# TensorE's place in a gather pipeline: a mark's own pairs taken at once at chosen marks, one more pair right behind new rows, and the first norm's rows behind the output projection

## The chip, the core and the metric

The kernel runs on one NeuronCore of a Trainium2 chip. The metric is the device time of one launch in microseconds (us), the median of several executions. The engines are called PE (TensorE), DVE (VectorE), ACT (ScalarE), POOL (GpSimd, which here does nothing but issue gathers) and SP (SyncE, which issues the weight loads).

## What is computed

One decoder layer over 1024 tokens of width 1024, all in float32: a combined input projection, sliding-window attention and a gated DeltaNet side by side, an output projection, a LayerNorm, then PEER (a product-key lookup of single-neuron experts), and a second LayerNorm.

```python
def reference(x, positions, w_in, ..., peer_w_query, peer_sub_keys, peer_u, peer_v, ln2_g, ln2_b):
    mix = hybrid_mixer(h, positions, w_in, attn_sinks, conv_w, a_log, dt_bias, dn_norm_g, w_out)
    h = layer_norm(DEEPNORM_ALPHA * h + mix, ln1_g, ln1_b)
    ffn = peer_ffn(h, peer_w_query, peer_sub_keys, peer_u, peer_v)
    h = layer_norm(DEEPNORM_ALPHA * h + ffn, ln2_g, ln2_b)

def one_block(xb):                       # 128 tokens
    q = (xb @ w_query).reshape(L, PEER_HEADS, 2, PEER_QUERY_DIM // 2)
    s = jnp.einsum('lhpd,hpkd->lhpk', q, sub_keys)
    vals, idx = lax.top_k(s, K)          # 16 of 128, for 8 heads x 2 halves
    ...
    best, pos = lax.top_k(cand, K)       # 16 of the 256 sums
    expert = jnp.take_along_axis(cidx, pos, axis=-1)
    gate = jax.nn.softmax(best, axis=-1)
    u = expert_u[expert]                 # 128 tokens x 128 experts x 1024
    v = expert_v[expert]
    h = jax.nn.gelu(jnp.einsum('ld,lhkd->lhk', xb, u), approximate=False)
    return jnp.einsum('lhk,lhkd->ld', (h * gate).astype(xb.dtype), v)
```

Every token has 128 experts of its own, and each brings a row of `u` and a row of `v`, 8 KB together. For all tokens that is 1.07 GB, which has to be gathered from memory.

## The kernel before

**Blocks.** The 1024 tokens are 8 blocks (`NB`) of 128. For each block all engines walk through the same function `mix(n, ...)`, each with its own part: rotary positions, attention, DeltaNet, output projection, first norm, queries, key scores and the choice of experts ("routing", on DVE, in four rounds `i` = 0 to 3). Weights come in 23 chunks of 1 MB, four of which stay in SBUF (`KEPT`); the other 19 are loaded anew for each block through two buffers (`chunk`), each load issued when PE has used the chunk two before it (`chunk_used`).

**Gathers.** A block has 128 gathers (`SLOTS`), one per choice of expert, each of 128 rows of 8 KB: 1 MB. POOL issues them in order into a ring of 8 places (`RING`), which is four pairs. Gather `j` may go out when PE has added gather `j - 8` (`added`), and the first of each 32 when DVE has written the expert numbers (`staged`, written in `expert_used`). 

**Pairs.** Two gathers are one pair (64 per block, `PAIRS`). For a pair DVE makes two dot products of the `u` rows with the tokens (L1421, the `CUSTOM_DVE` rows, `ring<-ring,x_pair`), ACT turns them by gelu and gate into a diagonal matrix (L994, L997, L1001, `diag`), and PE multiplies this with the `v` rows and sums in PSUM (L757, `expert_sum<-ring,diag`, eight instructions in the profile for a pair). Only then are two places of the ring free.

**Marks.** How pairs are woven into the mixer is a table. Each engine calls `mark(name)` at the same named steps, and there it does the pairs that the table gives to this name. `EARLIER` names the steps of block n at which pairs of block n-1 are done (49 pairs), `OWN` the later ones, from `top1` on, at which the block's own first 15 pairs are done, while routing goes on and PE already does the input projection of block n+1 (`in_chunk(n + 1, c)`). DVE and ACT do a mark's own pairs. PE stays one pair behind: its function is called with `b - 1`.

```python
def __call__(self, name):
    pairs, count = (self.own, OWN[name]) if name in OWN else (self.earlier, EARLIER[name])
    if pairs:
        pairs(self.done, self.done + count)
    self.done += count
```

**The turn from one block's pairs to the next's.** At `pick0` the first 32 expert numbers of the new block are there, and POOL may issue. PE does the last pair of the old block (`turn_over`), the four rows of the second norm's gain and shift (L514, `ln_row`, broadcast over the partitions by a matmul), and goes on. DVE waits for PE's last sum, reads the sums out of PSUM (`read_sums`, L1439), copies the gates into pair order (`by_pair`, L1401) and the new tokens' rows into `x_pair` (`stage_rows`, L1410). Pairs of the new block need `x_pair`.

**First norm.** Its gain and shift are spread by PE in the same way (`ln_row(LN1_G, ...)`, `ln_row(LN1_B, ...)`, L514), between the last DeltaNet step (mark `kv1`) and mark `dn`. Then PE waits for DVE's `dn_out`, transposes (L504), and does four output chunks (L485) with a mark behind each, `out0` to `out3`. DVE adds the residual, takes the statistics, asks ACT for the root, scales (needs the gain rows) and shifts (needs the shift rows).

## Time and profile before

| | us |
|---|---|
| median of 3 runs | 3309.68 |
| lowest, highest | 3298.28, 3327.20 |
| profiled execution, its own time | 3315.64 |
| profiled execution, span from first to last instruction | 3313.6 |

The page of the profile gives busy time by engine (PE 2454.9, DVE 2231.1, ACT 1142.5, POOL 1180.1 us) and says that 1254 MB were moved in 174885 packets, 379 GB/s over the span. Its DMA line shows the share of time in which the 16 DMA engines were busy, and its GB/s line what they moved. The two must be read together with a stretch in which the DMA engines never pause: there the same engines move 420 GB/s.

### The profile page before, as it was taken

What the parts mean: (1) busy time and instruction counts of PE and PEld (TensorE: products, weight loads), DVE (VectorE), ACT (ScalarE), POOL (GpSimd) and SP (SyncE); (2) the same over time, 40 slices, a digit from 0 to 9 for tenths busy, and PEclk for the clock granted to TensorE, in tenths of its full rate; (3) what the DMA queues carried; (4) which work ended last, traced back from release to release, by engine and by line L of the source; (5) the groups of instructions that cost most, each with busy time, mean ns of one, the idle gap of its engine ahead of it and who ended that gap; (6) DMA issues with size and microseconds to landing.
All of it is one profiled execution on the core that took longest, in us unless ns stands there. A gap on an engine that the chain in (4) does not pass through costs nothing.

```text
span 3313.6 us, 37482 instructions
## 1 busy us (share of the span) xinstructions
PE 2454.9 (74%) x11840; PEld 1381.2 (42%) x11840; DVE 2231.1 (67%) x5593; ACT 1142.5 (34%) x3499; POOL 1180.1 (36%) x1028
## 2 busy tenths in 40 slices
PE   7776778867888577876788677886788866775554
PEld 6663335533455233542346333552345523341111
DVE  3267765886558765687657876588656876569444
ACT  3213532235332443326232353233533253322222
POOL 0022443234432353224432344323453244323443
PEclk8788888988899898998989888997899879887777
DMA  8049999999999999999999999999999999989997
GB/s 327 7 198 405 393 419 399 378 389 411 408 385 412 379 408 405 382 406 382 420 395 378 400 391 407 400 392 389 411 407 397 402 390 417 389 356 351 419 420 316
DMA packets 174885, 1254.22 MB, mean 379 GB/s; under 512 B 20184, under 2 KB 20312, under 8 KB 23520
## 3 DMA queue, kind: packets, MB, share of 16 engines
q0 software_dynamic: 147456, 1073.81, 79.8%
q1 hardware_dynamic: 25056, 172.66, 12.6%
q10 hardware_dynamic: 2176, 5.36, 0.4%
q8 instruction: 95, 1.56, 0.2%
q14 instruction: 102, 0.84, 0.1%
HBM read 1247.56 MB, written 4.19 MB: 378 GB/s over the span
## 4 chain that ended last, share of the span: by engine, by line
DMA 33%; PE 33%; DVE 17%; ACT 9%; issue 5%; POOL 2%; ACTq 0%; DVEq 0%; POOLq 0%; SPq 0%
DMA ring<-in_uv,expert_used 21%; PE expert_sum L757 13%; DMA chunk<-in_weights 12%; PE bank L493 8%; DVE ring L1421 8%; PE bank L485 6%; ACT diag L1001 2%; POOL ring L445 2%; PE bank L499 1%; PE bank L586 1%; ACT L994 1%; ACT arena L861 1%; PE bank L504 1%; ACT h_raw L994 1%; DVE conv L1168 1%
## 5 line engine op out<-in xcount | busy, mean ns | idle before, releaser
L445 POOL DMA_INDIRECT ring<-in_uv,expert_used x1024 | 1179.9, 1152 | 2102.8 <-PE expert_sum L757 1600.8
L757 PE MATMUL expert_sum<-ring,diag 128*64 128x512 f32 x4096 | 1212.5, 721 | 646.0 <-ACT diag L1001 645.6
L1421 DVE CUSTOM_DVE_ANT_0 ring<-ring,x_pair 128x1024 f32<-128x1024 f32 x1024 | 1231.7, 1223 | 586.3 <-DMA ring<-in_uv,expert_used 581.3
L757 PEld LDWEIGHTS expert_sum<-ring,diag 128*64 128x64 f32 x4096 | 314.7, 156 | 1290.4 <-issue 1275.7
L994 ACT ACTIVATE h_raw<-h_raw 128x2 f32<-128x2 f32 x512 | 104.3, 204 | 1531.9 <-DVE h_raw L1421 1531.1
L1001 ACT ACTIVATE diag<-const,h_raw 128x64 f32<-128x64 f32 x1024 | 292.7, 332 | 0.0
L997 ACT ACTIVATE h_raw<-h_raw,gate_used 128x1 f32<-128x1 f32 x1024 | 245.6, 286 | 16.8
L493 PE MATMUL bank<-oT,chunk 128*128 128x128 f32 x1824 | 224.0, 282 | 33.0 <-DMA chunk<-in_weights 32.1
L493 PEld LDWEIGHTS bank<-oT,chunk 128*128 128x128 f32 x1824 | 213.3, 196 | 66.5 <-DMA chunk<-in_weights 39.6
L493 PE MATMUL bank<-o_cat,chunk 128*128 128x128 f32 x1376 | 172.4, 286 | 40.8 <-DMA chunk<-in_weights 40.6
L493 PEld LDWEIGHTS bank<-o_cat,chunk 128*128 128x128 f32 x1376 | 164.7, 200 | 76.6 <-DMA chunk<-in_weights 48.1
L1144 DVE MAX8 arena<-arena 128x8 f32<-128x128 f32 (+1 forms) x384 | 103.7, 325 | 46.5 <-ACT arena L953 41.3
L499 PEld LDWEIGHTS bank<-arena 128*128 128x128 f32 x768 | 97.7, 204 | 57.9 <-issue 50.8
L499 PE MATMUL bank<-arena 128*128 128x128 f32 x768 | 109.3, 295 | 5.5 <-DVE arena L1286 1.6
L949 ACT COPY arena<-bank 128x512 f32<-128x512 f32 x32 | 18.8, 586 | 265.2 <-PE bank L493 265.2
L485 PE MATMUL bank<-chunk,o_cat 128*128 128x256 f32 x352 | 86.4, 401 | 15.4 <-DMA chunk<-in_weights 15.4
L994 ACT ACT_TABLE_LOAD x72 | 92.4, 1283 | 3.8 <-DVE h_raw L1421 2.5
L485 PEld LDWEIGHTS bank<-chunk,o_cat 128*128 128x128 f32 x352 | 68.7, 200 | 36.7 <-issue 27.2
L1421 DVE DVE_READ_ACCUMULATOR2_ANT h_raw<- 128x1 f32 x1024 | 83.8, 82 | 0.0
L485 PE MATMUL bank<-kept,o_cat 128*128 128x256 f32 x256 | 74.3, 454 | 7.9 <-DMA kept<-in_weights 7.9
L1168 DVE SCALAR_TENSOR_TENSOR conv<-conv_in,conv_w,conv 128x128 f32<-128x128 f32 x288 | 77.7, 343 | 0.0
L485 PEld LDWEIGHTS bank<-kept,o_cat 128*128 128x128 f32 x256 | 58.0, 233 | 34.1 <-issue 22.9
(237 smaller groups left out, 2482.8 us busy)
## 6 DMA issues: line engine op xcount, KB each, us to landing
chunk<-in_weights SPq DMA_DIRECT2D x137, 1024.0 KB, 9.8
ring<-in_uv,expert_used POOLq DMA_INDIRECT x1024, 11.8
ring<-in_weights SPq DMA_DIRECT2D x15, 1024.0 KB, 20.3
o_cat<-in_xT SPq DMA_DIRECT2D x8, 512.0 KB, 11.7
kept<-in_weights SPq DMA_DIRECT2D x4, 1024.0 KB, 19.1
x<-in_x SPq DMA_DIRECT2D x8, 512.0 KB, 12.9
out<-oT ACTq DMA_DIRECT2D x8, 512.0 KB
sub_keys<-in_sub_keys ACTq DMA_DIRECT2D x1, 1024.0 KB
```

Source lines behind the costliest of these rows:

```text
L445: pool.indirect_dma_start(out=ring[:, (j % RING) * 2 * D:(j % RING + 1) * 2 * D], out_offset=None, in_=io["uv"], in_offset=bass.IndirectOf ...
L485: mm = pe.matmul(out, act[:, k, :], w[:, k, :], start=(k == 0), stop=(k == KT - 1))
L493: mm = pe.matmul(out, w[:, k, i * P:(i + 1) * P], act[:, k, :], start=(k == 0), stop=(k == KT - 1))
L499: mm = pe.matmul(out[:, hs], lhsT[:, hs], rhs[:, hs], start=True, stop=True)
L504: mm = pe.transpose(out[:, h * P:(h + 1) * P], in_[:, h * P:(h + 1) * P], ident)
L757: mm = pe.matmul(expert_sum[i][c * SPAN:(c + 1) * SPAN, :], diag[:, (j % DIAGS) * SPAN:(j % DIAGS + 1) * SPAN], ring3[:, j % RING, D + i * ...
L994: act.activation(h_raw[:, pair[0]:pair[1] + 1], h_raw[:, pair[0]:pair[1] + 1], ACT.Gelu).then_inc(gelued.sem, 1)
L997: act.activation(h_raw[:, j:j + 1], h_raw[:, j:j + 1], ACT.Copy, scale=gate_used[:, j:j + 1]).then_inc(weighted.sem, 1)
L1001: act.activation(diag[:, (j % DIAGS) * SPAN:(j % DIAGS + 1) * SPAN], C["halves"], ACT.Copy, scale=h_raw[:, j:j + 1]).then_inc(diag_ready.s ...
L1144: ins = dve.max(values[:, one[part]], one[2])
L1168: stt(out=convo[:, t, :], in0=conv3[:, t, k:k + P], scalar=conv_w[:, t * TAPS + k:t * TAPS + k + 1], in1=convo[:, t, :], op0=ALU.mult, op1 ...
L1421: dve.tensor_tensor_reduce(u, u, x_pair[:, (j % 2) * D:(j % 2 + 1) * D], 1.0, 0.0, ALU.mult, ALU.add, h_raw[:, j:j + 1]).then_inc(dotted.s ...
```

## The change

- `Marks` gets a list `prompt`. At a mark in this list PE does all pairs up to and with the mark's own; at any other mark it does all pairs before the mark's own and none of them. The list `PROMPT` has `gates, scores, taps2, norms, kv1, out0` to `out3, scale1, half_q, qu0` and all marks of `OWN`. DVE and ACT do what the table says, as before.
- The table: `dn` has one pair instead of two, and `OWN` has a new first mark `turned` with one pair, directly behind `turn_over` on DVE. PE does `in_chunk(n + 1, 0)` ahead of it.
- PE's turn: the last old pair comes ahead of the fourth key scores, not behind.
- DVE's turn: `by_pair` and half of the copies into `x_pair` (the half that `read_sums` doesn't read) are done before the wait for PE's last sum.
- The first norm's rows are made behind the fourth output chunk, ahead of mark `out3`.
- `diag` gets eight places instead of four; a constant, `same64`, is dropped for it, and one small matmul becomes two.

```diff
-DIAGS = 4
+DIAGS = 8
...
-    merge64=1, solve=2, ws0=1, kv0=2, ws1=1, kv1=1, dn=2, o_T=1, out0=1, out1=1, out2=1, out3=1,
+    merge64=1, solve=2, ws0=1, kv0=2, ws1=1, kv1=1, dn=1, o_T=1, out0=1, out1=1, out2=1, out3=1,
...
-OWN = {name: 1 for name in ("top1",) + NEXT_IN + AFTER_IN}
+OWN = {name: 1 for name in ("turned", "top1") + NEXT_IN + AFTER_IN}
+PROMPT = ("gates", "scores", "taps2", "norms", "kv1", "out0", "out1", "out2", "out3", "scale1", "half_q", "qu0") + tuple(OWN)
...
         if pairs:
-            pairs(self.done, self.done + count)
+            pairs(self.done, self.done + (count if name in self.prompt else 0))
...
-                pe.wait_ge(late_in, late)
                 pe.wait_ge(*o_copied.at(n, 2))
-                ln_row(LN1_G, 0, ln1_rows)
-                ln_row(LN1_B, 1, ln1_rows)
...
                     tokens_out(n, IN_CHUNKS + c, bank[3 + c // 2][:, (c % 2) * W:(c % 2 + 1) * W], oTv, early)
+                    if c == OUT_CHUNKS - 1:
+                        pe.wait_ge(late_in, late)
+                        ln_row(LN1_G, 0, ln1_rows)
+                        ln_row(LN1_B, 1, ln1_rows)
                     mark(f"out{c}")
...
                 mark("pick0")
+                turn_over(n)
                 score_keys(3)
-                turn_over(n)
+                second_norm_rows(n)
+                if onward:
+                    in_chunk(n + 1, 0)
+                mark("turned")
                 mark("top1")
-                for c, name in enumerate(NEXT_IN):
-                    if onward:
+                for c, name in enumerate(NEXT_IN, 1):
+                    if onward and c < IN_CHUNKS:
                         in_chunk(n + 1, c)
                     mark(name)
...
-            mix(0, Marks(own=lambda a, b: experts(0, b - 1)), lambda n: None, early=True)
+            mix(0, Marks(own=lambda a, b: experts(0, b), prompt=PROMPT), lambda n: None, early=True)
...
             def turn_over(n):
 
-                dve.wait_ge(*chunk_used.at(n, CHUNKS))
-                read_sums(n - 1)
-                stage_rows(n)
+                if n > 0:
+                    dve.wait_ge(*added.at(n - 1, 2 * PART))
+                by_pair(gate_used, gate, 0, PART)
+                stage_rows(n, False)
+                if n > 0:
+                    dve.wait_ge(*chunk_used.at(n, CHUNKS))
+                    read_sums(n - 1)
+                stage_rows(n, True).then_inc(rows_staged.sem, 1)
```

**Where instructions stand.** First PE, from the last DeltaNet matmul of a block to the first query chunk. L673/L674 are the DeltaNet output, L757 (after: L763) pairs, L514 the norm's rows, L504 transposes, L485 output chunks, L493 a query chunk; a pair is x4 here. Before:

```order
L674 MATMUL bank<-conv,arena 128x128
L757 MATMUL expert_sum<-ring,diag 64x512 x4
L514 MATMUL bank<-k_keys,const 128x512 x4
L757 MATMUL expert_sum<-ring,diag 64x512 x8
L504 MATMUL bank<-const,o_cat 128x128 x8
L757 MATMUL expert_sum<-ring,diag 64x512 x4
L485 MATMUL bank<-kept,oT 128x256 x8
L757 MATMUL expert_sum<-ring,diag 64x512 x4
L485 MATMUL bank<-kept,oT 128x256 x8
```

After:

```order
L675 MATMUL bank<-conv,arena 128x128
L763 MATMUL expert_sum<-ring,diag 64x512 x8
L504 MATMUL bank<-const,o_cat 128x128 x8
L763 MATMUL expert_sum<-ring,diag 64x512 x4
L485 MATMUL bank<-kept,oT 128x256 x8
L763 MATMUL expert_sum<-ring,diag 64x512 x8
L485 MATMUL bank<-kept,oT 128x256 x8
```

Between the DeltaNet and the transposes two pairs stand instead of three, and no rows; behind the first output chunk stand two pairs instead of one.

Second PE, at the turn, from the last query chunks to the second chunk of the next block's input projection (L718, after L720, are key scores; `o_cat` is the next block's input). Before:

```order
L493 MATMUL bank<-oT,chunk 128x128 x32
L757 MATMUL expert_sum<-ring,diag 64x512 x4
L718 MATMUL bank<-sub_keys,arena 128x128 x4
L757 MATMUL expert_sum<-ring,diag 64x512 x4
L514 MATMUL bank<-k_keys,const 128x512 x4
L485 MATMUL bank<-kept,o_cat 128x256 x8
L757 MATMUL expert_sum<-ring,diag 64x512 x4
L485 MATMUL bank<-kept,o_cat 128x256 x8
```

After:

```order
L493 MATMUL bank<-oT,chunk 128x128 x32
L763 MATMUL expert_sum<-ring,diag 64x512 x8
L720 MATMUL bank<-sub_keys,arena 128x128 x4
L514 MATMUL bank<-k_keys,const 128x512 x4
L485 MATMUL bank<-kept,o_cat 128x256 x8
L763 MATMUL expert_sum<-ring,diag 64x512 x8
L485 MATMUL bank<-kept,o_cat 128x256 x8
```

The last old pair moved ahead of the key scores, and two new pairs stand between the first two input chunks instead of one. Later in the same run PE has five pairs in a row, not four, ahead of the transposes of `rope`.

Third DVE at the turn (L1439, after L1447, reads the sums; L1144 to L1153, after L1153 to L1162, are the first half of routing round 1). Before:

```order
L1392 TENSOR_TENSOR gate<-gate,small 128x32
L1439 SCALAR_TENSOR_TENSOR oT<-x_pair,expert_sum 64x512 x4
L1401 COPY gate_used<-gate 64x16 x4
L1410 COPY x_pair<-x 64x1024 x4
L1144 MAX arena<-arena 128x8 x4
L1151 MAX_INDEX arena<-arena 128x8 x4
L1153 MATCH_REPLACE arena<-arena 128x128 x4
L1421 ISA ring,h_raw<-ring,x_pair 128x1024
```

After:

```order
L1402 TENSOR_TENSOR gate<-gate,small 128x32
L1411 COPY gate_used<-gate 64x16 x4
L1418 COPY x_pair<-x 64x1024 x2
L1447 SCALAR_TENSOR_TENSOR oT<-x_pair,expert_sum 64x512 x4
L1418 COPY x_pair<-x 64x1024 x2
L1429 ISA ring,h_raw<-ring,x_pair 128x1024
```

The gate copies and two row copies moved ahead of the sums, and the first new pair ahead of the routing.

## Rows read from the trace of the kernel before

**Rows 1.** The page: busy time by engine
```profile
PE 2454.9 (74%) x11840; PEld 1381.2 (42%) x11840; DVE 2231.1 (67%) x5593; ACT 1142.5 (34%) x3499; POOL 1180.1 (36%) x1028
```

**Rows 2.** Windows over blocks: engines' busy us, PE clock, DMA share, GB/s
```profile
592.83:2946.12 2353.29, 1798.11 (x8882) 1021.37 (x8880) 1662.64 (x4177) 862.43 (x2628) 883.94 (x768) 0.89 0.98 398
206.32:592.83 386.51, 294.35 (x1482) 168.64 (x1480) 268.20 (x677) 138.37 (x428) 144.47 (x128) 0.88 0.98 402
...
2946.12:3075.00 128.88, 72.97 (x224) 22.75 (x224) 108.07 (x328) 32.74 (x111) 46.81 (x44) 0.71 0.89 341
```

**Rows 3.** Windows within one block (gathers of block 3 and the next turn)
```profile
1395.00:1426.00 31.00, 24.81 (x123) 15.89 (x121) 29.58 (x95) 9.84 (x27) 7.95 (x7) 0.93 0.98 379
1426.00:1504.00 78.00, 51.67 (x278) 31.27 (x279) 63.95 (x210) 26.02 (x80) 22.14 (x22) 0.88 1.01 420
1504.00:1515.00 11.00, 11.00 (x44) 5.12 (x43) 10.82 (x30) 4.70 (x18) 4.29 (x5) 0.79 0.56 205
...
1674.00:1700.00 26.00, 26.00 (x108) 15.33 (x105) 10.59 (x19) 6.88 (x27) 11.45 (x10) 0.90 0.98 377
...
1769.90:1792.00 22.10, 19.32 (x80) 12.79 (x80) 12.78 (x42) 3.50 (x8) 8.71 (x8) 0.84 0.94 376
1792.00:1827.00 35.00, 30.42 (x171) 20.36 (x172) 33.50 (x106) 13.12 (x38) 10.82 (x10) 0.90 0.91 349
```

**Rows 4.** Who waited for whom: us in total, times, longest
```profile
POOL ring L445 <- PE expert_sum L757: 1600.8, 442, 15.1
```

**Rows 5.** Timeline of PE behind the own pairs: start, us, idle before
```profile
1502.79 1.89 PE L548 MATMUL bank<-const,arena 128*64 128x128 f32 x8 [7.95 <-DVE arena L1188]
...
1505.04 7.08 PE L757 MATMUL expert_sum<-ring,diag 128*64 128x512 f32 x24
```

**Rows 6.** Timeline of ACT and POOL at the same place
```profile
1498.68 0.57 ACT L1001 ACTIVATE diag<-const,h_raw 128x64 f32<-128x64 f32 x2
...
1509.49 0.94 POOL L445 DMA_INDIRECT ring<-in_uv,expert_used  x1 [10.66 <-PE expert_sum L757]
```

**Rows 7.** Timeline of DVE and PE from DeltaNet's end to the queries
```profile
1661.97 3.70 PE L514 MATMUL bank<-k_keys,const 8*128 8x512 f32 x8
...
1673.29 3.68 PE L757 MATMUL expert_sum<-ring,diag 128*64 128x512 f32 x8 [4.11 <-ACT diag L1001]
...
1680.84 3.72 PE L485 MATMUL bank<-kept,oT 128*128 128x256 f32 x16
...
1690.01 1.94 PE L757 MATMUL expert_sum<-ring,diag 128*64 128x512 f32 x8
...
1734.45 1.94 PE L757 MATMUL expert_sum<-ring,diag 128*64 128x512 f32 x8
...
1668.94 0.69 DVE L1316 TENSOR_TENSOR o_cat<-arena,small 128x512 f32<-128x512 f32 x1
...
1683.03 0.57 ACT L1001 ACTIVATE diag<-const,h_raw 128x64 f32<-128x64 f32 x2
...
1725.03 0.57 ACT L1001 ACTIVATE diag<-const,h_raw 128x64 f32<-128x64 f32 x2
```

**Rows 8.** Timeline of PE and DVE at the turn
```profile
1784.30 5.41 PE L485 MATMUL bank<-kept,o_cat 128*128 128x256 f32 x16
1794.31 3.68 PE L757 MATMUL expert_sum<-ring,diag 128*64 128x512 f32 x8 [4.60 <-ACT diag L1001]
...
1780.90 2.78 DVE L1439 SCALAR_TENSOR_TENSOR oT<-x_pair,expert_sum 64x512 f32<-64x512 f32 x4 [7.88 <-PE expert_sum L757]
...
1784.44 2.79 DVE L1410 COPY x_pair<-x 64x1024 f32<-64x1024 f32 x4
...
1790.50 1.23 DVE L1421 CUSTOM_DVE_ANT_0 ring<-ring,x_pair 128x1024 f32<-128x1024 f32 x1
```

**Rows 9.** Timeline of POOL at the turn
```profile
1769.90 1.17 POOL L445 DMA_INDIRECT ring<-in_uv,expert_used  x1 [15.67 <-DVE expert_used L1401]
...
1798.76 1.07 POOL L445 DMA_INDIRECT ring<-in_uv,expert_used  x1 [15.06 <-PE expert_sum L757]
```

More of the change, by code:

```diff
@@ L762, in experts @@
                                 mm.then_inc(added.sem, 1)
-                taken[0] = last
+                taken[0] = max(taken[0], last)
             def second_norm_rows(n):
-                pe.wait_ge(*key_scores_c.at(n, 4))
+                if n == 0:
+                    return
+                if n < NB:
+                    pe.wait_ge(*key_scores_c.at(n, 4))
                 ln_row(LN2_G, 2, ln2_rows)
@@ L974, in mix @@
                 key_scores_out(3)
+                mark("turned")
                 mark("top1")
-                for c, name in enumerate(NEXT_IN):
+                for c, name in enumerate(NEXT_IN, 1):
                     if onward:
@@ L1383, in mix @@
                         turn_over(n)
+                        mark("turned")
                 weights_out(n, 2, slice(2, PH))
@@ L1402, in by_pair, with stage_rows @@
                 return ins
-            def stage_rows(n):
-                by_pair(gate_used, gate, 0, PART)
-                dve.wait_ge(*sums_read.at(n, 0))
+            def stage_rows(n, own):
                 for s in range(2):
-                    for c in range(2):
-                        ins = dve.tensor_copy(x_pair[s * SPAN:(s + 1) * SPAN, c * D:(c + 1) * D], x1[c * SPAN:(c + 1) * SPAN, :])
-                ins.then_inc(rows_staged.sem, 1)
+                    c = s if own else 1 - s
+                    ins = dve.tensor_copy(x_pair[s * SPAN:(s + 1) * SPAN, c * D:(c + 1) * D], x1[c * SPAN:(c + 1) * SPAN, :])
+                return ins
             def experts(n, first, last):
@@ L1441, in read_sums @@
                 ins.then_inc(sums_read.sem, 1)
+                dve.wait_ge(*sums_read.at(n, 1))
             def second_stats(n):
```

24 lines of the change are left out of this document (11 added, 13 removed).

## The prediction, made before the changed kernel ran

> **What bounds the kernel now.** I read the busy times first: no engine is busy for more than 74% of the span [rows 1], so none is the bound. Then the windows. Where the DMA engines never pause they move 420 GB/s, in the window of 78 us [rows 3]. Over the six blocks from 592.83 to 2946.12 us it is 398 GB/s [rows 2]. So gathers and weights bound the kernel, and what can be won at unchanged traffic is the time in which the DMA engines run dry: 2353.29 x (1 - 398/420) = 123 us, 20.5 per block. In the first block it is 386.51 x (1 - 402/420) = 16.6, and in the first 129 us of the last block's gathers 128.88 x (1 - 341/420) = 24.2 [rows 2].
>
> Next, where in a block they run dry. The same sum for windows of one block [rows 3]: 1395 to 1426, behind the turn, 3.0 us (and 5.9 at the next turn, 1792 to 1827; mean 4.5); 1504 to 1515, between the own pairs and the next block's attention, 5.6; 1674 to 1700, output projection, 2.7; 1769.90 to 1792, the new block's first gathers, 2.3. Together 15.1 of the 20.5. Small dips elsewhere make up the other 5.4, and I count no gain for them.
>
> Then who holds the ring. POOL waited 1600.8 us for PE's sums [rows 4]. Mostly that is harmless, since gathers already out keep the engines busy. It costs when the four pairs' worth of cover (8 MB, 20 us at 420 GB/s) is used up. A pair that PE takes later than ACT has it ready shortens this cover by so much.
>
> **The change, part by part.** I call a stretch's dry time its shortage.
>
> *Own pairs' end (shortage 5.6).* ACT had the last own pair's matrices ready at 1499.25 [rows 6], but PE, one pair behind, takes it only at `rope`. It waits 7.95 us for DVE's rotated rows and reaches the pair at 1505.04 [rows 5]. POOL's next gather goes out at 1509.49, after 10.66 us [rows 6], and just there the rate is 205 GB/s [rows 3]. Now the pair is taken at `pick3`. Even at the slow 3.68 us for a pair after idling [rows 8] its places are free at about 1503, so the gather goes out some 6 us earlier. On top of this the own part has 16 pairs instead of 15, so one more gather pair (5.0 us of traffic at 420 GB/s) is already out. 6 + 5 is more than 5.6; I take 5.0 back, because later gathers follow at DVE's pace.
>
> *The turn (shortage 4.5).* DVE idles 7.88 us for PE's last sum, then reads 2.78, copies gates, copies rows 2.79, does half a routing round, and starts the first new pair at 1790.50 [rows 8]. The gate copies (0.7, the gap between the two rows) and half of the row copies (1.4) go into those 7.88 us, and the routing (3.2, from 1787.3 to 1790.5) comes behind the pair. The first new pair starts at 1780.90 + 2.78 + 1.4 = 1785.1, 5.4 us earlier. PE takes it behind last sum, scores, norm rows and one chunk; it stood waiting 4.60 us for this pair [rows 8], after two chunks of 2.7 each at 5.41 for both. So PE can be there at about 1788.5, when ACT is ready as well. The first freed place goes to POOL about 5 us before 1798.76 [rows 9]. Each later own pair is one mark ahead too, at the price of one pair more (2.4 us) on a DVE that is busy for 33.50 of 35 us there [rows 3]. 5 against a shortage of 4.5: I take 3.5. Moving the last old pair ahead of the key scores gains DVE little, since ACT's matrix for it was the wait. The fourth scores come about 3 us later, and only routing round 3 reads them, far behind.
>
> *First gathers (shortage 2.3).* They wait for DVE's expert numbers, 15.67 us up to 1769.90 [rows 9], and nothing in routing is taken out. But DVE does pairs between its steps and waits for their landing. PE takes the pair ready at 1725.60 only at 1734.45 [rows 7]; with `half_q` prompt it does so behind the first query chunk, some 5 us sooner, and a later gather leaves sooner too. Against it, the second query chunk starts 1.94 us later, and at `qu0` PE may wait some 2 us for ACT. I take 1.0, between nothing and 2.3.
>
> *Output projection (shortage 2.7).* PE does the norm's rows (3.70) and two pairs and waits 4.11 us for the second, so the transposes start at 1673.29 + 3.61 = 1676.9, though DVE's `o_cat` was there at 1669.6 [rows 7]. Now one of these pairs and the rows are gone from there, and `dn` takes nothing of its own: the transposes can start 7 us earlier. Behind the output chunks the lag goes: a pair ready at 1683.60 was taken at 1690.01 [rows 7], 6.4 us late. The rows' 3.70 us now lie behind the fourth chunk, where DVE adds a residual half, takes statistics, does one pair and waits for ACT's root before it wants them; nothing is exposed, and if this cover were gone it would be 3.70. I take 2.0.
>
> *The rest.* Eight places of `diag`: ACT's wait for a free one does not show in the trace, so 0. One more small matmul per block: under 0.3 us, in PE's wait. DVE's added wait for its own sums: 0.1. In the own part itself the list changes nothing but names: the order of in-chunks and pairs is the same, one pair ahead.
>
> *Sum.* 5.0 + 3.5 + 1.0 + 2.0 = 11.5 per block, 69 for six. The first block has no turn from old pairs but the other three: 8. In the last block's beginning no weights flow and the spacing of DVE's marks keeps the rate down; it has the turn and an extra early pair: 6. Together 83 us. From the profiled execution's 3315.64 (span 3313.6 and 2.0 around it) that gives 3233. It lies 6 us over the median of the runs, 3309.68, with which the result is compared: 3309.7 - 83 = **3227**.
>
> **A rule of the skill weighed.** The pages give this traffic another bound: the Trainium skill, "DMA: Bandwidth & Descriptors", section Bandwidth, says that some 358 GB/s per core bind between memory and SBUF. By that the DMA engines would have no dry time and the change would give 0. The trace disagrees, with 420 GB/s over 78 us, so it gets no chance.
>
> **The rivals.**
> 1. *The chain of the engines is next.* Gathers leave earlier, but a stage is then as long as DVE's and PE's work in it. For it: DVE's 33.50 of 35 us behind the turn. Against it: PE's and DVE's waits for rows that stand all over the block. Half of the gain stays: 3309.7 - 42 = 3268.
> 2. *Nearly all shortages go*, since being one pair ahead carries into stretches I counted at nothing: 17 of 20.5 per block, x6 = 102, plus 18: 3190.
> 3. *Slower: PE waits for each own pair at the four output chunks and at the two query marks, and its clock falls.* A pair after such a wait took 3.68 us against 1.94, and two chunks 5.41 against 3.72 [rows 7, 8]. At the four chunks that is 4 x (1.74 + 1.69) = 13.7. At the query marks it is 2 x 1.74 + 2 for waiting + 3.3 for the two chunks = 8.8. Together 22.5 per block on the path to the routing. If all of it is exposed, 7 blocks x 22.5 - 83 = +75: 3384. It decides against the change from 12 us exposed per block on. Against it: PE had these pairs' matrices 6 to 9 us before it took them, so it will mostly not wait. The Trainium skill, "TensorE: Matmul & The Clock Gate", section HAM oscillation, says that idle gaps between bursts let the clock drop to half; the rows at both durations agree.
> 4. *It doesn't do what it says.* At the marks of the own part this is so already, and if PE were late everywhere for its work and not for the list, prompt marks would move nothing. The turn and `pick3` would still give 8.5 per block: 3309.7 - 60 = 3250, inside rival 1's part of the range.
>
> **Chances.** Forecast as worked out (3205 to 3255, with rival 4) 0.60; rival 1 0.22; rival 2 0.13; slower 0.05. The range leaves out rival 3 and the ends: 3190 to 3277. A measurement of this kernel tells about 1% from no change, 33 us. Faster by more than that (under 3277): all of the forecast and rival 2, and half or more of rival 1, 0.86. Within 1%: 0.10. Slower: 0.04.
>
> **What would show it.** Right: GB/s over the middle six blocks near 410 instead of 398; no window like 1504 to 1515 with half the rate; POOL's gather behind the own pairs waiting under 6 us; the first new pair on DVE some 4 us behind its reading of the sums; transposes of the output projection right behind `o_cat`. Wrong: PE's waits for ACT at L763 grow in sum, with a lower clock, DVE waiting longer for output chunks and first key scores (rival 3), or the windows' rate still below 405 with DVE full (rival 1).

## The result, and the profile after

The changed kernel takes 3369.1 us (median of 4 runs, 3366.78 to 3385.12) against 3305.64 for the kernel before beside it (4 runs, 3298.28 to 3327.20): ratio 1.0184, interval 1.0154 to 1.0214. The forecast was 3227, faster. It is wrong in its direction, not only in a size. One execution of all those below, of e4 (3394.91 us at a granted clock of 0.765), is in a slower state of the chip, stands in no ratio and is not read.

The page after: busy time by engine, and the two costliest groups (busy us, mean ns of one, idle before, releaser).

```profile
PE 2492.1 (74%) x11856; PEld 1403.8 (42%) x11856; DVE 2231.0 (66%) x5593; ACT 1136.6 (34%) x3499; POOL 1162.2 (35%) x1028
...
L445 POOL DMA_INDIRECT ring<-in_uv,expert_used x1024 | 1162.0, 1135 | 2175.7 <-PE expert_sum L763 1752.8
L763 PE MATMUL expert_sum<-ring,diag 128*64 128x512 f32 x4096 | 1226.7, 732 | 759.0 <-ACT diag L1010 758.6
```

Busy times are those of [rows 1] within 2%, so nothing became a full engine. POOL waits 152 us longer for PE's sums than in [rows 4], where it should have waited less. The windows of the kernel after say the same (columns as in [rows 2]: the six middle blocks, 78 us of the own part, and two windows behind the own pairs):

```profile
590.60:2997.60 2407.00, 1840.75 (x8890) 1044.51 (x8890) 1662.32 (x4177) 855.99 (x2625) 868.94 (x768) 0.87 0.96 389
...
1440.00:1518.00 78.00, 59.58 (x323) 38.06 (x321) 53.37 (x177) 18.51 (x73) 21.91 (x21) 0.89 0.94 378
1519.00:1532.00 13.00, 8.42 (x23) 2.72 (x24) 12.51 (x38) 7.07 (x13) 4.20 (x4) 0.51 1.01 420
1536.00:1547.00 11.00, 10.24 (x40) 4.65 (x36) 10.24 (x23) 2.98 (x13) 4.27 (x4) 0.89 0.82 316
```

389 GB/s over six blocks instead of 398 [rows 2]. The hole behind the own pairs, 205 GB/s [rows 3], is indeed gone (420, then 316 in the 11 us from 1536). But the own part itself, which ran at 420 GB/s before [rows 3], is at 378. This is the worst of the six middle blocks; taken from 30 us behind the last copy into `x_pair` to 13 us ahead of PE's transposes of the rotated rows, the mean of the six is 418 GB/s before and 401 after. So a part of the loss begins there. The waits of the kernel after (us in total, times, longest; L824 and L844 are ACT's copies of finished input chunks out of PSUM):

```profile
ACT h_raw L1003 <- DVE h_raw L1429: 1246.2, 332, 11.4
...
DVE ring L1429 <- DMA ring<-in_uv,expert_used: 581.1, 432, 6.0
...
ACT conv_in L824 <- PE bank L493: 247.4, 24, 12.1
...
ACT z L844 <- PE bank L485: 82.7, 8, 12.9
```

The same lines before were 1531.1 (L994), 581.3, 92.0 in 18 waits (L816) and 34.7 (L836). ACT now waits 155 us longer for input chunks and 285 us less for dot products: dot products lie finished while ACT stands at a chunk. DVE's wait for landings has not moved at all. Now PE's timeline in that place (L763 a pair, L493 a chunk; in brackets the idle time before, and its releaser), then ACT's:

```profile
1452.95 3.84 PE L493 MATMUL bank<-o_cat,chunk 128*128 128x128 f32 x32
1459.95 3.63 PE L763 MATMUL expert_sum<-ring,diag 128*64 128x512 f32 x8 [3.16 <-ACT diag L1010]
1463.52 3.84 PE L493 MATMUL bank<-o_cat,chunk 128*128 128x128 f32 x32
1467.29 1.94 PE L763 MATMUL expert_sum<-ring,diag 128*64 128x512 f32 x8
1469.15 3.84 PE L493 MATMUL bank<-o_cat,chunk 128*128 128x128 f32 x32
```

```profile
1456.83 0.59 ACT L824 COPY conv_in<-bank 128x512 f32<-128x512 f32 x1 [10.44 <-PE bank L493]
1457.45 1.28 ACT L829 ACTIVATE conv<-conv_in,conv_w 128x128 f32<-128x128 f32 x4
1458.63 0.19 ACT L1003 ACTIVATE h_raw<-h_raw 128x2 f32<-128x2 f32 x1
...
1459.47 0.33 ACT L1010 ACTIVATE diag<-const,h_raw 128x64 f32<-128x64 f32 x1
...
1473.03 0.59 ACT L824 COPY conv_in<-bank 128x512 f32<-128x512 f32 x1 [12.08 <-PE bank L493]
```

This is a **lock step**. PE ends a chunk at 1456.8. ACT was waiting for just this chunk (10.44 us), copies it, does the convolution's taps, and only then makes the matrices of a pair whose dot products DVE had finished earlier. PE waits 3.16 us for them before it may begin the next chunk, and takes the pair in 3.63 us instead of 1.94. Then ACT waits for PE again, 12.08 us. Two marks take 16.2 us (1456.83 to 1473.03). Before, in the same place of the same block, only weights held PE up (PE, then ACT):

```profile
1447.42 3.84 PE L493 MATMUL bank<-o_cat,chunk 128*128 128x128 f32 x32
1451.19 1.94 PE L757 MATMUL expert_sum<-ring,diag 128*64 128x512 f32 x8
1455.06 3.84 PE L493 MATMUL bank<-o_cat,chunk 128*128 128x128 f32 x32 [1.93 <-DMA chunk<-in_weights]
```

```profile
1445.66 0.59 ACT L816 COPY conv_in<-bank 128x512 f32<-128x512 f32 x1 [4.92 <-PE bank L493]
...
1458.93 0.59 ACT L816 COPY conv_in<-bank 128x512 f32<-128x512 f32 x1 [6.58 <-PE bank L493]
```

13.3 us for two marks. Of the 2.9 us more, 1.2 are PE's wait (3.16 for ACT instead of 1.93 for weights), and 1.7 are the pair behind the wait, at 3.63 instead of 1.94. The line that closes the loop is in the part of the diff that concerns ACT:

```diff
                 mark("turned")
                 mark("top1")
-                for c, name in enumerate(NEXT_IN):
+                for c, name in enumerate(NEXT_IN, 1):
                     if onward:
                         in_out(n + 1, c)
                     mark(name)
```

ACT's copy of chunk c moved one name earlier, and PE takes that name's own pair right behind chunk c. So each pair needs ACT, ACT needs the chunk ahead of the pair, and the next chunk needs the pair.

### The profile page after: what moved, and what is told of

Read it like the earlier page. It is cut to its first block, busy times and chain, and to the rows that moved or that the text cites. A ratio compares the mean times of both kernels' runs of the same rounds, so it can differ in the third digit from the quotient of the medians.

```text
span 3368.1 us, 37520 instructions
## 1 busy us (share of the span) xinstructions
PE 2492.1 (74%) x11856; PEld 1403.8 (42%) x11856; DVE 2231.0 (66%) x5593; ACT 1136.6 (34%) x3499; POOL 1162.2 (35%) x1028
## 4 chain that ended last, share of the span: by engine, by line
PE 45%; DMA 21%; DVE 16%; ACT 11%; issue 5%; POOL 2%; ACTq 0%; DVEq 0%; POOLq 0%; SPq 0%
PE expert_sum L763 18%; DMA ring<-in_uv,expert_used 17%; PE bank L493 11%; DVE ring L1429 8%; PE bank L485 7%; DMA chunk<-in_weights 3%; ACT diag L1010 2%; POOL ring L445 2%; ACT L1003 1%; PE bank L586 1%; PE bank L514 1%; ACT arena L869 1%; PE bank L560 1%; PE bank L499 1%; ACT h_raw L1003 1%
## 5 line engine op out<-in xcount | busy, mean ns | idle before, releaser
L445 POOL DMA_INDIRECT ring<-in_uv,expert_used x1024 | 1162.0, 1135 | 2175.7 <-PE expert_sum L763 1752.8
L763 PE MATMUL expert_sum<-ring,diag 128*64 128x512 f32 x4096 | 1226.7, 732 | 759.0 <-ACT diag L1010 758.6
L763 PEld LDWEIGHTS expert_sum<-ring,diag 128*64 128x64 f32 x4096 | 326.3, 159 | 1413.1 <-issue 1401.8
L1006 ACT ACTIVATE h_raw<-h_raw,gate_used 128x1 f32<-128x1 f32 x1024 | 245.6, 286 | 16.7
L493 PE MATMUL bank<-oT,chunk 128*128 128x128 f32 x1824 | 227.8, 287 | 25.5 <-DMA chunk<-in_weights 24.7
L493 PEld LDWEIGHTS bank<-oT,chunk 128*128 128x128 f32 x1824 | 219.7, 202 | 58.1 <-issue 46.6
L493 PEld LDWEIGHTS bank<-o_cat,chunk 128*128 128x128 f32 x1376 | 162.0, 197 | 42.2 <-issue 35.7
L493 PE MATMUL bank<-o_cat,chunk 128*128 128x128 f32 x1376 | 170.0, 283 | 1.4 <-DMA chunk<-in_weights 1.4
L1153 DVE MAX8 arena<-arena 128x8 f32<-128x128 f32 (+1 forms) x384 | 103.7, 325 | 53.5 <-ACT arena L961 48.6
L824 ACT COPY conv_in<-bank 128x512 f32<-128x512 f32 x24 | 14.1, 587 | 247.4 <-PE bank L493 247.4
L485 PE MATMUL bank<-chunk,o_cat 128*128 128x256 f32 x352 | 90.5, 415 | 0.3 <-DMA chunk<-in_weights 0.3
L1334 DVE SCALAR_TENSOR_TENSOR x<-x,bank 128x512 f32<-128x512 f32 x16 | 11.0, 688 | 115.6 <-PE bank L485 115.6
L485 PEld LDWEIGHTS bank<-chunk,o_cat 128*128 128x128 f32 x352 | 71.5, 209 | 23.9 <-issue 13.4
L485 PE MATMUL bank<-kept,o_cat 128*128 128x256 f32 x256 | 74.3, 455 | 7.7 <-DMA kept<-in_weights 7.7
```

Source lines behind the costliest of these rows:

```text
L445: pool.indirect_dma_start(out=ring[:, (j % RING) * 2 * D:(j % RING + 1) * 2 * D], out_offset=None, in_=io["uv"], in_offset=bass.IndirectOf ...
L485: mm = pe.matmul(out, act[:, k, :], w[:, k, :], start=(k == 0), stop=(k == KT - 1))
L493: mm = pe.matmul(out, w[:, k, i * P:(i + 1) * P], act[:, k, :], start=(k == 0), stop=(k == KT - 1))
L763: mm = pe.matmul(expert_sum[i][c * SPAN:(c + 1) * SPAN, :], diag[:, (j % DIAGS) * SPAN:(j % DIAGS + 1) * SPAN], ring3[:, j % RING, D + i * ...
L1006: act.activation(h_raw[:, j:j + 1], h_raw[:, j:j + 1], ACT.Copy, scale=gate_used[:, j:j + 1]).then_inc(weighted.sem, 1)
L1153: ins = dve.max(values[:, one[part]], one[2])
```

## The experiments

Fifteen kernels ran. Each ratio is to the kernel before, from runs in turn with it on the same chip. The e and f runs were on one chip, the g runs on a second, the h runs on a third; one and the same kernel came out at 1.0039 as e4 and at 1.0028 as g4, so a distance between such groups is known to some 0.1% less well. The table orders them by what they contain; "12 marks" are the entries of `PROMPT` from `gates` to `qu0`.

| kernel | what it has | ratio | interval |
|---|---|---|---|
| f2 | first norm's rows moved | 1.0013 | 0.9996 to 1.0029 |
| f3 | turn alone | 0.9953 | 0.9930 to 0.9977 |
| f4 | turn, norm's rows, own pairs directly behind their chunks, eight places of `diag` | 0.9966 | 0.9946 to 0.9985 |
| h1 | f4 + lock step | 1.0078 | 1.0047 to 1.0109 |
| g4, e4 | f4 + extra pair | 1.0028, 1.0039 | 1.0003 to 1.0053, 1.0021 to 1.0058 |
| e3 | f4 + extra pair + lock step | 1.0109 | 1.0088 to 1.0130 |
| e1 | f4 + extra pair + 12 marks | 1.0096 | 1.0066 to 1.0127 |
| e2 | as after, but PE one pair behind at `NEXT_IN` | 1.0142 | 1.0116 to 1.0167 |
| after | all | 1.0184 | 1.0154 to 1.0214 |
| f1 | 12 marks alone | 1.0118 | 1.0090 to 1.0146 |
| g3 | f1, ACT's pair of `qu0` ahead of its score copy | 1.0090 | 1.0055 to 1.0124 |
| g2 | 10 of the 12 (without `half_q`, `qu0`) | 1.0053 | 1.0032 to 1.0075 |
| g1 | `half_q`, `qu0` | 1.0004 | 0.9979 to 1.0029 |
| h2 | `out0` to `out3`, `scale1` | 1.0009 | 0.9993 to 1.0025 |
| h3 | `gates`, `scores`, `taps2`, `norms`, `kv1` | 0.9998 | 0.9984 to 1.0013 |

How long the parts of a block took, in us (my table, from the starts and ends of single rows of the timelines, mean of five block periods: last copy into `x_pair`, last rotated row, `dn_out`, first transpose of `x1`, first key scores, first gather of the next block, last copy into `x_pair`). Each column is one profiled execution, and these lie up to 0.5% off their medians: g4's is its fastest (3310.7 us against 3323.8), g1's and g2's are 10 and 12 us under theirs, f1's is 16 us over (3368.8 against 3353.2).

```
                 before  after   f3     f4     h1     g4     e1     f1     g1     g2
own part         107.6  115.0  106.7  107.7  113.5  112.0  110.5  107.2  107.5  107.4
mixer to dn_out  168.8  171.7  170.5  168.0  166.4  168.6  172.1  170.2  169.1  167.6
to x1 transposed  50.4   48.9   50.3   49.8   49.7   47.0   48.8   52.0   47.7   51.7
to key scores 0   13.3   14.9   13.6   13.7   13.9   13.7   14.9   16.2   15.2   13.5
to first gather   37.0   34.1   37.0   37.3   37.0   38.4   34.8   33.3   33.7   38.1
to x_pair         15.2   17.3   13.1   12.6   13.5   11.8   16.7   20.5   18.8   14.9
```

**e1: the lock step taken out of the changed kernel.**

```diff
-                for c, name in enumerate(NEXT_IN, 1):
+                for c, name in enumerate(NEXT_IN):
                     if onward:
                         in_out(n + 1, c)
```

> The changed kernel with one edit on ACT alone: its part of the next block's input projection (the copies out of PSUM) stands one mark later again, as in the kernel before; PE's order is that of the changed kernel. Theory A (lock step: in the own part PE waits for a pair whose matrix ACT makes only after it has copied the chunk that PE has just done; PE and ACT then go round a ring of 8.1 us per mark): the part from the new rows to the rotated rows of the next block falls from 115.0 to 108 us or less, ACT's wait for PE before the convolution copies from 247 to under 120 us, and the time to 3300 to 3325. Theory B (the prompt marks of the earlier part, where PE waits for ACT): 3360 or more. Theory C (DVE is the bound in the own part and has one pair more there): 3365 to 3375.

1.0096 instead of 1.0184, the own part 110.5 us instead of 115.0, and ACT's wait at `conv_in` back from 247.4 to 114.0 us. About half of the loss is the lock step's. The other half is something else, which none of the three theories on record had as its size: 3348 us lies above theory A's range.

**e2: PE one pair behind at `NEXT_IN`, ACT as in the changed kernel.**

```diff
-PROMPT = (..., "half_q", "qu0") + tuple(OWN)
+PROMPT = (..., "half_q", "qu0") + ("turned", "top1") + AFTER_IN
```

> The changed kernel with the eleven marks of NEXT_IN taken out of the prompt list, so that between input chunks PE takes the pair of the mark before; ACT as in the changed kernel. Theory A: the ring is open here too, 3305 to 3330, own part near 108 us. Theory B: 3360 or more. Theory C: 3365 to 3375.

1.0142. It breaks the circle at its other end, and half as much comes back as in e1 (3355 us, again outside theory A's range). Every own pair is then taken a chunk later; whether that is why not more comes back stays open.

**e3: the 12 early marks taken back, the lock step left.**

```diff
-mix(n, Marks(lambda a, b: experts(n - 1, b), lambda a, b: experts(n, b), prompt=PROMPT), turn_over)
+mix(n, Marks(lambda a, b: experts(n - 1, b - 1), lambda a, b: experts(n, b)), turn_over)
```

> The changed kernel with PE one pair behind at all marks of the earlier part, as before; own part, turn and the norm's rows as changed. Theory A: the own part stays at 115 us; the earlier part moves by some 3 us per block one way or the other, 3345 to 3390. Theory B: most of the loss is gone, under 3330. Theory C: as theory A.

1.0109: the 12 marks cost 0.75% in the changed kernel. They were to bring the better part of two terms of my sum.

**e4 and g4: both taken back** (the edits of e1 and e3 together; g4 is the same kernel again).

> Both edits together: ACT's copies one mark later, PE one pair behind in the earlier part. What is left of the change is the pair directly upon new rows, DVE's turn, the last own pair taken at its mark, and the norm's rows. Theory A: 3290 to 3325, and the distance to the kernel with the first edit alone says what the prompt list is worth in the earlier part. Theory B: as the kernel with PE one pair behind alone, under 3330. Theory C: 3360 or more.

> The kernel of e4 once more (changed kernel without the lock step and without the twelve early marks), for more runs and a usable profile. It differs from f4 (0.9966) by the pair directly upon the new rows alone. If the extra pair costs: ratio 1.002 to 1.006 as in e4, and the profile shows where; if e4's difference was chance: 0.996 to 0.999.

1.0039 and 1.0028. The two costs add (0.9% and 0.7%). What is left of the change is still no gain. The profile of this kernel in the table is g4's.

**f4: no extra pair.**

```diff
-OWN = {name: 1 for name in ("turned", "top1") + NEXT_IN + AFTER_IN}
+OWN = {name: 1 for name in ("top1",) + NEXT_IN + AFTER_IN}
```

with `dn=2`, on e4.

> The changed kernel with the lock step and the twelve prompt marks of the earlier part taken back (as in e4), and without the pair directly upon the new rows: the own part has 15 pairs, begins at top1, and dn takes two pairs again. TensorE takes each own pair directly behind its chunk. Against e4 (1.0039 of before): theory C, the extra pair costs VectorE some 2.9 us per block in the own part and brings 3 back later, so no difference, 1.002 to 1.006. If the extra pair is what is left of the loss, ratio 0.995 to 1.000; if it is the gain that the prediction named, 1.007 or more.

0.9966, and g4 with the pair 1.0028: the pair directly upon the new rows costs 0.6%, some 20 us. In the table the own part is 4.3 us longer with it, and 2.8 come back between `dn_out` and the transposes, where a pair is missing. I had expected the two to cancel. This distance is between two chips, but e4, on f4's own chip, is at 1.0039.

**h1: the lock step alone, on f4** (e1's edit the other way round, without an extra pair).

> f4 (0.9966 of before) with one thing more: in the own part ScalarE's in_out of chunk c stands ahead of the pair that TensorE takes directly behind chunk c, as in the changed kernel (one name earlier in ScalarE's list). Theory A (lock step: ScalarE waits for the chunk before it makes the matrices, TensorE waits for the matrices before the next chunk): some 0.8% on f4, ratio 1.003 to 1.007, the stretch up to the rotated rows 4 to 8 us longer per block. If e1's gain of 0.9% came from something else in the changed kernel (its extra pair): ratio 0.995 to 0.999.

1.0078 against 0.9966, 1.1% for one number in ACT's list, a little more than the range on record (1.003 to 1.007). Waits of f4, then of h1:

```profile
ACT h_raw L1001 <- DVE h_raw L1426: 1488.9, 403, 11.2
...
PE expert_sum L762 <- ACT diag L1008: 680.6, 269, 7.8
...
ACT conv_in L823 <- PE bank L493: 85.1, 16, 11.0
```

```profile
ACT h_raw L1001 <- DVE h_raw L1426: 1237.8, 342, 11.0
PE expert_sum L762 <- ACT diag L1008: 757.7, 291, 6.9
...
ACT conv_in L823 <- PE bank L493: 238.7, 23, 13.1
```

The same signature as in the changed kernel, in the same sizes. The granted clock of the six middle blocks is 0.89 in f4 and in h1, so PE is not slower on the whole. Inside a round it can be. PE's pairs behind two of h1's waits:

```profile
1441.93 1.94 PE L762 MATMUL expert_sum<-ring,diag 128*64 128x512 f32 x8 [3.16 <-ACT diag L1008]
...
1456.66 2.80 PE L762 MATMUL expert_sum<-ring,diag 128*64 128x512 f32 x8 [3.17 <-ACT diag L1008]
```

The first round, from one of ACT's copies to the next (1438.80 to 1453.53), takes 14.7 us, the second (to 1469.66) 16.1: its pair takes 2.80 us and its next chunk 4.59 instead of 3.84. In f4 the same copies are 13.4 and 13.2 us apart. So of up to 2.9 us per round about half is the bare round trip, and the rest, where it comes, is PE slower right behind its wait.

**f2: the norm's rows alone.** PE's two `ln_row` calls move from ahead of `mark("dn")` to behind the fourth output chunk, as in the change.

> The kernel before, with the first norm's row matmuls alone moved behind the fourth output chunk. The prediction's view: 3.70 us less ahead of the transposes and their cover behind the chunk, so up to 7 x 2 = 14 us faster, ratio 0.996 to 1.000. If the cover is gone there (VectorE wants the rows at once), each of seven blocks gives back up to 3.7 us behind the chunk: ratio 1.000 to 1.004.

1.0013, no difference: the rows' place was worth nothing before and is worth nothing now.

**f3: the turn alone.**

```diff
+                    dve.wait_ge(*added.at(n - 1, 2 * PART))
+                by_pair(gate_used, gate, 0, PART)
+                stage_rows(n, False)
                     read_sums(n - 1)
-                stage_rows(n)
+                stage_rows(n, True).then_inc(rows_staged.sem, 1)
...
-                score_keys(3)
                 turn_over(n)
+                score_keys(3)
+                second_norm_rows(n)
```

> The kernel before, with the turn alone: VectorE copies gates and the first half of the new rows ahead of its wait for the last sum, and TensorE takes the last old pair ahead of the fourth key scores and the second norm's rows behind them; no pair directly upon the new rows. The prediction's turn term, without the routing that moved behind the pair (3.2 of 5.4 us): 2.1 us of 7.9 us of waiting per turn, 5 to 15 us in all, ratio 0.995 to 0.999. If this work never stood on the path (gathers already out cover it), ratio 0.999 to 1.001. If the order of TensorE costs (fourth scores 3 us later are wanted at once), over 1.001.

0.9953, the fastest of all 17 kernels: 3298.98 us beside 3313.31. From the first gather to the new rows a block takes 13.1 us instead of 15.2. At the six middle turns DVE's first new pair starts 7.5 us behind its reading of the sums instead of 9.6, and POOL's first gather upon a new pair's sum leaves 14.0 to 15.0 us behind it instead of 17.5 to 17.9. Which of the two, DVE's order or PE's, brings the gain was not tried apart.

**f1: the 12 marks alone, on the kernel before.**

```diff
+PROMPT = ("gates", "scores", "taps2", "norms", "kv1", "out0", ..., "scale1", "half_q", "qu0")
...
-            pairs(self.done, self.done + count)
+            pairs(self.done, self.done + (count if name in OWN or name in self.prompt else 0))
```

(PE's functions get `b` for earlier pairs and still `b - 1` for own ones.)

> The kernel before, with one thing of the change: at the twelve marks of the earlier part that the change lists (gates to qu0) TensorE takes the mark's own pair; the own part, the turn and the norm's rows stay as before. Theory B (TensorE waits for the pair just handed over and the attention's chain behind it comes later; about 22 us between the runs with and without these marks): ratio 1.005 to 1.009, 3330 to 3342 us, with the query stretch longer than before. The prediction's view (places of the ring come free earlier): 15 to 20 us faster, ratio 0.995. If the marks cost only beside the changed own part, the ratio is within 0.998 to 1.002.

1.0118, more than the 0.7% in the changed kernel. From `x1` transposed to the new rows a block of the profiled execution takes 70.0 us instead of 65.5. PE and ACT of f1 at `qu0` (L719 key scores, L950 and L954 ACT's copies of queries and of scores):

```profile
1770.78 1.16 PE L719 MATMUL bank<-sub_keys,arena 128*128 128x128 f32 x8 [1.63 <-ACT arena L950]
1773.79 3.68 PE L758 MATMUL expert_sum<-ring,diag 128*64 128x512 f32 x8 [1.86 <-ACT diag L1002]
1777.40 8.53 PE L494 MATMUL bank<-oT,chunk 128*128 128x128 f32 x64
```

```profile
1771.97 0.58 ACT L954 COPY arena<-bank 128x512 f32<-128x512 f32 x1 [1.25 <-PE bank L719]
...
1773.08 0.57 ACT L1002 ACTIVATE diag<-const,h_raw 128x64 f32<-128x64 f32 x2
```

A second loop of the same kind: ACT's copy of the first key scores stands ahead of the pair, and the pair, now prompt, ahead of the next query chunks. Scores at 1770.78, next chunk at 1777.40: 6.6 us. Before, scores at 1733.36 and next chunk at 1737.45, 4.1 us. This made theory Q of the next three runs.

**g1, g2, g3: the query marks alone; the other ten alone; f1 with ACT's pair ahead of its score copy.**

Against f1:

```diff
-PROMPT = (... all 12 ...)
+PROMPT = ("half_q", "qu0")                     # g1; g2 has the other ten
...
                 queries_out(0)
+                mark("qu0")                    # g3, ACT
                 key_scores_out(0)
-                mark("qu0")
```

> The kernel before, where TensorE takes the mark's own pair at half_q and qu0 alone (two of f1's twelve marks). Theory Q (in f1 TensorE waits at qu0 for matrices that ScalarE makes only behind its copy of the first key scores, 1.86 us, and takes the pair in 3.68 instead of 1.94; every later query chunk and key score follows later): most of f1's loss, ratio 1.005 to 1.011, VectorE's idle time in the query stretch some 5 us per block longer than before. If the loss comes from the output chunks, ratio within 1.002. The prediction's view: first gathers' term, 1.0 per block, ratio 0.998.

> The other ten of f1's twelve marks (gates, scores, taps2, norms, kv1, the four output chunks, scale1), on the kernel before. Theory Q: little, ratio 0.998 to 1.003. If the output chunks carry f1's loss: 1.008 or more. The prediction's view (6 us of lag gone behind the output chunks): ratio 0.994 to 0.998.

> f1 with one thing more: ScalarE makes the matrices of qu0's pair ahead of its copy of the first key scores, so that they are ready when TensorE comes. Theory Q, round trip: TensorE's wait at qu0 goes and with it a good part of f1's loss, ratio 1.002 to 1.008 instead of 1.0118. If not the wait but the pair between the two first query chunks or the marks ahead of them cost, it stays at 1.009 to 1.014.

Theory Q falls as the main cause: the query marks alone cost nothing (1.0004). In the table g1 does lose 2.2 us between transposes and new rows, but the stretch ahead of them is 2.7 shorter. The other ten cost 0.5%, between the ranges of both theories. Opening the small loop (g3) gives 0.3% back, inside the two intervals, so it is suggested at most.

**h2, h3: the ten split once more**, by `PROMPT` alone.

> The kernel before, where TensorE takes the mark's own pair at out0 to out3 and scale1 alone (five of g2's ten). If the output stretch carries g2's 1.0053: ratio 1.003 to 1.007. If the places that come free earlier are worth something by themselves: 0.995 to 0.999. If g2's loss is in the other five: 0.999 to 1.002.

> The kernel before, where TensorE takes the mark's own pair at gates, scores, taps2, norms and kv1 alone (the other five of g2's ten). If they carry g2's 1.0053: ratio 1.003 to 1.007; the pair at scores and norms then stands ahead of a step that VectorE waits for. If the output marks do: 0.998 to 1.002.

1.0009 and 0.9998. Three groups of marks cost nothing each that could be told from zero; two of them together 0.5%, all three 1.2%. No single place carries the loss. The numbers come from three chips; the 1.2% is far more than that could explain, the 0.5% less clearly.

## Why the prediction was wrong

**The step that failed** is the sentence "In the own part itself the list changes nothing but names: the order of in-chunks and pairs is the same, one pair ahead". It holds for PE's list and was never laid beside ACT's. Before, PE took a pair one chunk after ACT had made it, and this lag kept the two engines apart. Without it, and with ACT's copies a name earlier, they meet at every second mark, 16.2 us for two instead of 13.3. It measures 1.1% (h1 against f4), 0.9% (after against e1), 0.8% (e3 against g4): some 26 to 37 us, half of the result, and it stood in no rival.

That is the largest single cost, not the whole error. The way from the forecast's -83 us to the measured +61 (1.84%) is 144 us. Of these 72 are gain that did not come (f4 is 11 us faster, not 83), 29 the lock step (after to e1), 22 the twelve early marks (e1 to g4), 21 the extra pair (g4 to f4).

**The bound.** "What can be won at unchanged traffic is the time in which the DMA engines run dry" was the premise of all four terms, and it doesn't hold for the largest, the end of the own pairs. f4 shows it best, since it has the prompt own pairs and none of the costs. Windows of the kernel before, behind the own pairs of block 3 (the window 1504 to 1515 stands in [rows 3]); the last one is the whole stretch:

```profile
1515.00:1535.00 20.00, 12.83 (x45) 4.05 (x43) 19.43 (x47) 7.39 (x27) 9.62 (x8) 0.83 1.01 420
1535.00:1555.00 20.00, 15.06 (x73) 7.66 (x73) 11.44 (x22) 16.81 (x41) 8.30 (x8) 0.91 1.01 418
1555.00:1575.00 20.00, 14.36 (x66) 6.31 (x67) 12.72 (x23) 14.02 (x34) 9.92 (x10) 0.91 1.00 385
1490.00:1575.00 85.00, 58.15 (x235) 25.05 (x236) 67.88 (x160) 52.27 (x137) 37.12 (x32) 0.83 0.95 383
```

and of f4, 14 us earlier on its clock: the same four pieces, the hole first, and the whole stretch:

```profile
1490.00:1501.00 11.00, 9.16 (x40) 4.54 (x40) 10.96 (x25) 3.85 (x15) 5.76 (x5) 1.00 0.97 370
1501.00:1521.00 20.00, 11.84 (x42) 4.03 (x40) 18.69 (x49) 10.14 (x34) 9.36 (x8) 0.83 0.90 363
1521.00:1541.00 20.00, 16.07 (x76) 7.77 (x76) 9.98 (x19) 16.93 (x37) 6.88 (x6) 0.91 0.96 378
1541.00:1561.00 20.00, 12.81 (x62) 5.96 (x60) 16.08 (x29) 11.19 (x32) 10.23 (x10) 0.91 0.98 398
1476.00:1561.00 85.00, 58.22 (x242) 25.02 (x238) 69.12 (x160) 50.45 (x133) 37.29 (x33) 0.85 0.96 383
```

The hole of 205 GB/s is filled to 370, and the next 60 us fall from 420, 418, 385 to 363, 378, 398. Over the 85 us it is 383 both times, no more than it was. The other blocks agree. In the 12 us from PE's transposes of the rotated rows on, the mean of six blocks is 228 GB/s before and 332 in f4; in the 85 us from 13 us ahead of these transposes on, it is 380 and 375. The engines' chain through the mixer takes as long as before (168.8 and 168.0 us in the table) and hands over so many pairs in it; gathers that leave earlier are gathers that are missing later. My indicator for this ("POOL's gather behind the own pairs waiting under 6 us") came true in f4 and in the changed kernel, and meant nothing. At the turn it is otherwise. There f3 makes a step shorter, DVE's way from the sums to the first new pair, by 2.1 us, and the traffic that it fills in stays won: from 15 us ahead of the last copy into `x_pair` to 40 us behind it, the mean of six blocks is 374 GB/s before and 389 in f3. That a hole is worth its size only where a step of the block gets shorter is my reading of these two places; no run tests it by itself. In the changed kernel DVE's wait for landings is the old 581 us.

So of the sum's terms:

- *Own pairs' end, 5.0.* The gathers do leave earlier, as said, but this is worth nothing: own pairs directly behind their chunks (f4, with the norm's rows and the places of `diag` besides) bring no more than the turn without them (f3).
- *Turn, 3.5.* The DVE half is right. In the changed kernel the first new pair starts 4.24 us behind the reading of the sums, where 4.2 was worked out:

```profile
1405.77 2.78 DVE L1447 SCALAR_TENSOR_TENSOR oT<-x_pair,expert_sum 64x512 f32<-64x512 f32 x4 [7.78 <-PE expert_sum L763]
1408.58 1.39 DVE L1418 COPY x_pair<-x 64x1024 f32<-64x1024 f32 x2
1410.01 1.22 DVE L1429 CUSTOM_DVE_ANT_0 ring<-ring,x_pair 128x1024 f32<-128x1024 f32 x1
```

  The PE half falls short. PE at the same turn:

```profile
1407.41 5.85 PE L514 MATMUL bank<-k_keys,const 8*128 8x512 f32 x8 [0.68 <-ACT arena L961]
1413.19 6.59 PE L485 MATMUL bank<-kept,o_cat 128*128 128x256 f32 x16
1419.71 3.65 PE L763 MATMUL expert_sum<-ring,diag 128*64 128x512 f32 x16
```

  It reaches the pair 13.9 us behind the sum's reading (1419.71 - 1405.77), not 7.6; before it was 13.4 (1794.31 - 1780.90, [rows 8]). This is the worst of the six middle turns of the kernel after: they have 10.6 to 13.9, mean 12.0, where the kernel before has 13.4 each time. I had read the x16 of [rows 8] as "two chunks of 2.7 each"; it is one chunk (8 matmuls in the code, 16 in the trace), so the whole 5.41 us stand ahead of the pair and not half. And at most of these turns the norm's rows and the chunk take longer than in the sum, here 5.85 and 6.59 us where [rows 7, 8] have 3.70 and 5.41. So POOL's first gather upon a new pair's sum leaves 13.3 to 16.7 us behind the reading, mean 14.7, instead of 17.7: 3 us earlier, and not 5. In this block the traffic drops behind the turn all the same:

```profile
1419.00:1431.00 12.00, 8.73 (x38) 4.70 (x38) 11.14 (x39) 6.22 (x12) 4.25 (x4) 0.93 0.72 276
```

  What the term is worth without its pair directly upon the new rows is in f3: 0.47%, 15.6 us over seven turns, 2.2 each.
- *One pair more in the own part.* I priced it at 2.4 us on DVE and let "5 against a shortage of 4.5" cover it. It costs some 20 us in all, 2.9 per turn: about the priced 2.4, with nothing to set against it.
- *First gathers, 1.0.* Nothing (g1).
- *Output projection, 2.0.* The transposes start right behind `o_cat`, as said:

```profile
1702.51 1.94 PE L504 MATMUL bank<-const,o_cat 128*128 128x128 f32 x8 [2.21 <-DVE o_cat L1325]
```

  and it brings nothing (f2, h2). In the changed kernel the stretch is 1.5 us shorter, though it has a pair fewer, and the next three together are 0.8 longer.

**The rivals.** Rival 1 (the chain of the engines is next) names the reason for the missing gain, and "half of the gain stays" was still far too kind: a fifth of it, in f3. Rival 3 (PE waits for prompt pairs and takes them slowly) had the right sign and a chance of 0.05. That its 3384 lies near the measured 3369 is luck: it was priced from waits at the output chunks and the query marks, and of the 72 us lost above, 50 are the lock step's and the extra pair's, both in the own part. In f1, which has these marks alone, PE's wait for matrices is 647.5 us, as before (645.6). Its argument against itself, that PE "had these pairs' matrices 6 to 9 us before it took them", is true of the lag as it was; the same lag was what made it true. Its place is only partly right: in block 3 of the changed kernel PE doesn't wait at `out0` to `out2`, but 2.39 us at `out3` (behind the norm's rows), 6.02 at `scale1` and 1.86 at `qu0`.

**The rule of the skill** about 358 GB/s, which I gave no chance, would have meant no gain from filling holes. f4's small gain looks like it, but not for that reason: f4 still averages 400 GB/s over its six middle blocks, and the kernel before holds 420 for 78 us. The Trainium skill itself says so on another page, "HBM Reference", section Specifications (TRN2): a core that streams alone goes well above its share. The trace agrees, with 420.

**What stays open.** Why marks that cost nothing in groups of two and five cost 1.2% together. Pairs get longer along with it: the mean matmul of a pair is 721 ns before, 723 in g1, 725 in h2, 731 in h3, 736 in g2 and here in f1,

```profile
L758 PE MATMUL expert_sum<-ring,diag 128*64 128x512 f32 x4096 | 1249.8, 744 | 647.9 <-ACT diag L1002 647.5
```

with a granted clock of 0.86 over its six middle blocks instead of 0.89 [rows 2]. PE is busy 58 us longer than before, in a profiled execution whose span is 53 us longer. But this is one of f1's two slowest executions, with its lowest clock (0.841 over the whole span; the other five have 0.848 to 0.859), and its median is only 40 us above the kernel before. Slower matmuls are large enough to be the cause, and other runs speak against it: h3 has 731 ns and no loss, and of two kernels on one chip g1 has a median clock of 0.857 and costs nothing, g2 one of 0.859 and costs 0.5% (the kernel before beside them: 0.868). So the cause is open.

## What to carry to other kernels

A lag of one item between two engines that walk through the same list is a buffer. Before removing it, lay both engines' lists side by side and look for a loop: A's next step behind an item that B makes, and B's item behind a copy that waits for A's last step. Then ask of every hole in the transfers which step of the chain gets shorter when it is filled; if none does, expect the bytes to be missing in the next hundred microseconds, as here in the next 60. And try the parts of a bundle alone: here the part that gains (the turn, 0.5%) was hidden under three that lose (0.9, 0.7 and 0.6%).

## What was unexpected of the hardware

At the turn of the changed kernel PE's clock fell while PE was at work. The windows of the kernel after, the two halves of 1395 to 1419:

```profile
1395.00:1407.00 12.00, 10.33 (x73) 7.27 (x71) 4.04 (x13) 3.25 (x8) 5.54 (x6) 1.00 0.97 380
1407.00:1419.00 12.00, 11.59 (x22) 6.62 (x23) 11.71 (x35) 2.55 (x11) 1.30 (x2) 0.57 1.01 421
```

In the first 12 us PE was busy for 10.33 at the full clock, its waits there were 1.40 and 0.68 us, and then the granted clock was 0.57, near the lower of its two levels (1.2 of 2.4 GHz), for 12 us of almost unbroken work (11.59 busy): the norm's rows took 5.85 us instead of 3.70 [rows 7], the chunk 6.59 instead of 5.41 [rows 8]. The Trainium skill, "TensorE: Matmul & The Clock Gate", section HAM oscillation, has idle gaps lower the clock; the trace has only small ones here. It is no single case: at the six middle turns the same rows take 3.69 to 5.85 us after, 3.69 to 4.29 before. From the rows ahead of a stretch I could not have told at which clock it would run, and a sum that takes 3.70 or 5.41 from another place carries this error.
